# Moving the one-step recurrence and half of the key pages inside a hybrid decoder layer

## What is computed

```python
h = rmsnorm(x); z = h @ w_in                     # 25 column slots of 128, then the value and forget columns
# A: forgetting attention, 4 heads x 64; for the samples over 64 pages of 128 cached keys and values each
s = q @ k.T * 0.125 + c_q - c_k;  o_a = softmax(s) @ v        # c = running sum of the log forget gates
# B: RWKV-7 recurrence, 4 heads x 64, over the prompt in chunks and over the samples step by step
s_kk = sum_k(s * kk);  s = s * w - s_kk * (kk * a) + v * k;  o_b = sum_k(s * r)
o_b = group_norm(o_b) + bonus
# C: causal pooling, D: depthwise convolution module
y = rmsnorm(x + concat(o_a*silu(g_a), o_b*silu(g_b), o_c*silu(g_c), o_d*silu(g_d)) @ w_out)
```

## Time and profile before

| | us |
|---|---|
| median of 3 runs (1960.63 to 1970.27) | 1962.02 |
| the profiled execution | 1961.91 |
| its span from the first to the last instruction | 1960.1 |

### The profile page before, as it was taken

The page is one execution under the profiler, slowest core; times in us unless marked ns, Lnnn a source line. Parts: engine busy times, 40 slices in busy tenths (PEclk is TensorE's granted clock), DMA queues, the critical chain, the costliest instruction groups (busy, mean ns, idle before and its releaser), DMA issues.

```text
span 1960.1 us, 34623 instructions
## 1 busy us (share of the span) xinstructions
PE 1801.5 (92%) x14642; PEld 1092.4 (56%) x14642; DVE 817.9 (42%) x1662; ACT 478.5 (24%) x855; POOL 170.1 (9%) x220
## 2 busy tenths in 40 slices
PE   6999999999999999979999997887788786999997
PEld 3555555555554556746776775666667342444442
DVE  4450799732213350036556533444434864111112
ACT  4301100010526231125554531111112231100000
POOL 1000000011000005600000000000000001111110
PEclk9999999999999999989999998998989798999999
DMA  6222321385230535141100057777776536878782
GB/s 224 78 105 80 118 87 64 121 196 158 92 120 33 204 153 206 50 152 39 54 1 1 2 175 224 221 236 218 213 226 193 226 100 230 296 272 277 277 297 74
DMA packets 149269, 298.62 MB, mean 152 GB/s; under 512 B 23301, under 2 KB 119349, under 8 KB 130742
## 3 DMA queue, kind: packets, MB, share of 16 engines
q1 hardware_dynamic: 126602, 152.65, 24.7%
q0 software_dynamic: 18240, 115.82, 17.3%
q10 hardware_dynamic: 4272, 27.93, 3.6%
HBM read 234.66 MB, written 63.92 MB: 152 GB/s over the span
## 4 chain that ended last, share of the span: by engine, by line
PE 58%; DVE 17%; SPq 15%; issue 4%; DMA 3%; ACT 3%; POOL 0%; ACTq 0%; DVEq 0%
PE psum L756 23%; PE psum L1257 12%; SPq L525 12%; DVE big L1647 8%; PE psum L908 6%; PE psum L948 4%; PE psum L841 3%; PE psum L919 3%; PE psum L895 2%; SPq L521 2%; PE psum L788 1%; ACT big L1326 1%; PE psum L1242 1%; DMA rkv<-big 1%; DVE big L2029 1%
## 5 line engine op out<-in xcount | busy, mean ns | idle before, releaser
L756 PE MATMUL psum<-big,wbuf 128*128 128x416 f32 x1920 | 675.4, 513 | 3.9 <-DVE big L1577 3.4
L756 PEld LDWEIGHTS psum<-big,wbuf 128*128 128x128 f32 x1920 | 365.0, 190 | 310.7 <-issue 309.0
L948 PE MATMUL psum<-big 64*64 64x64 f32 (+2 forms) x6496 | 269.6, 281 | 48.8 <-DMA big<-in_k_pages 34.0
L948 PEld LDWEIGHTS psum<-big 64*64 64x64 f32 (+1 forms) x6496 | 190.0, 132 | 140.1 <-issue 69.5
L1295 ACT ACTIVATE zst<-psum 128x416 f32<-128x416 f32 x125 | 64.0, 516 | 540.7 <-PE psum L756 540.6
L1257 PE MATMUL psum<-big 128*128 128x512 f32 (+1 forms) x408 | 181.8, 595 | 0.0
L720 POOL DMA_INDIRECT big<-in_cache_v,pidx x64 | 60.7, 949 | 1027.2 <-PE psum L948 1020.5
L1647 DVE SCALAR_TENSOR_TENSOR big<-big,pars 128x2048 f32<-128x2048 f32 x120 | 148.2, 1298 | 1.1
L1257 PEld LDWEIGHTS psum<-big 128*128 128x128 f32 (+1 forms) x408 | 76.2, 187 | 101.4 <-issue 101.4
L2116 DVE TENSOR_TENSOR zst<-zst,psum 128x1024 f32<-128x1024 f32 (+1 forms) x17 | 20.7, 1221 | 224.5 <-PE psum L1257 224.5
L1555 ACT ACTIVATE big<-zst 128x1024 f32<-128x1024 f32 (+1 forms) x17 | 18.0, 1057 | 299.8 <-DVE zst L2116 299.8
(11 more groups left out here) (238 smaller groups left out, 1818.2 us busy)
## 6 DMA issues: line engine op xcount, KB each, us to landing
big<-in_k_pages SPq DMA_DIRECT2D x352, 128.0 KB, 2.3
zT<-zst ACTq DMA_DIRECT2D x25, 1040.0 KB, 6.5
zst<-in_k_pages SPq DMA_DIRECT2D x160, 128.0 KB, 2.4
wbuf<-in_w_slots SPq DMA_DIRECT2D x24, 512.0 KB, 4.5
big<-zT POOLq DMA_DIRECT2D x11, 1024.0 KB, 5.6
rwS<-big POOLq DMA_DIRECT2D x8, 1024.0 KB, 4.2
big<-rwS SPq DMA_DIRECT2D x8, 1024.0 KB, 5.9
zst<-in_x_prompt SPq DMA_DIRECT2D x16, 512.0 KB, 9.2
```

What stands on the lines that cost most here:

```text
L756: last = nc.tensor.matmul(psum[:, m % CHUNKS, 0:CW], w[:, k, :], hT[:, k, c * CW:(c + 1) * CW], start=(k == 0), stop=(k == KT - 1))
L948: return nc.tensor.matmul(out, l, r, start=start, stop=stop, skip_group_check=True)
```

## The change

**The recurrence of the samples** now runs inside the projection. The host hands the state over turned (`state_T`), so that the sum over k is a sum over partitions: `sample_step(i)` makes `s_kk` with 32 small products, whose stationary side is one column broadcast to 64x64, and the output of the step before with 32 products of one column. That is five calls: before the last piece of slot 23 and before value rows 0, 2, 4 and 6. VectorE keeps per step four operations of 128x1024, after four that prepare the values. The value rows of the samples are turned on TensorE after slot 21, copied by ScalarE in slot 22, stored by four ScalarE transfers to `zsD` and loaded, spread over 64 partitions, by SyncE. The keys and queries of attention are loaded after this is done, since they use the same memory. The value rows use PSUM banks 0 to 4 in place of 5 to 7.

**Half of the key steps** (16 of 32) now stand in attention, after items 6, 8, ..., 24 and then 25 to 30. They have one buffer (`k_early`, 2 MB), so that SyncE loads the next 16 pages when the step before has been scored. In the recurrence each pair keeps two steps, with the ring of three. To make room, the gates of attention come tile by tile: before item j+3 SyncE loads its 128x128 gate into one of four small buffers, and it stores the result of each item by itself. The queries of the samples are laid out at item 1 (`decode_queries`, at item 31 before), and the scans go to items 3, 11, 17, 19, 21, 23, 25 and 27.

**The tail** after the pairs: the norm comes first, piece by piece with both channel halves, so that `mixb_ready` rises ten times; two blocks of probabilities are turned after its first pass and six after its third, then ten value tiles run back to back. `project` takes the products of mixer B last.

```diff
+v_row = [area(HT + 13010 + i * 1024, 1024) for i in range(DEC_SEQ)]
+s_wkv = [area(HT + 17106, 1024), area(HT + 18130, 1024)]
+s_tmp = area(HT + 19154, 1024)
+v_turned = pars[0:SMP, 339:595].rearrange("p (h t x) -> p h t x", h=2, t=2)
+o_smp = sb("o_smp", [P, 2, SMP])
...
+KEYS_AT = (6, 8, 10, 12, 14, 16, 18, 20, 22, 24, 25, 26, 27, 28, 29, 30)
+SUMS_AT = (3, 11, 17, 19, 21, 23, 25, 27)
+KEARLY = len(KEYS_AT)
+KPAIR = (KSTEPS - KEARLY) // NPAIR
...
+    sp.wait_ge(v_spread, 16 * DEC_SEQ)
+    sp.dma_start(s_wkv[0], I['state_T']).then_inc(s_in, 16)
+    for i in range(DEC_SEQ):
+        sp.dma_start(v_row[i], zsD[i].unsqueeze(1).to_broadcast([2, 64, 1024])).then_inc(x_in[i], 16)
...
+    sp.wait_ge(s_done, 1)
+    sp.dma_start(O['wkvT_sample'], s_wkv[0]).then_inc(wkv_stored, 16)
+    sp.wait_ge(wkv_stored, 16)
...
+    def gate_store(j):
+        i, pr = ITEMS[j]
+        sp.wait_ge(o_read, j + 1)
+        sp.dma_start(mixT[MIX_A + pr][:, i * P:(i + 1) * P], gate_a[j % 4]).then_inc(mixa_stored[j % 2], 16)
+        if j + 3 < len(ITEMS):
+            if j > 0:
+                sp.wait_ge(mixa_stored[1 - j % 2], 16 * ((j + 1) // 2))
+            gate_load(j + 3)
...
+        if k < KEARLY:
+            if k > 0:
+                sp.wait_ge(sc_mm, k)
+        elif k - KEARLY >= NRING:
...
+    for j in range(len(ITEMS) - 2):
+        if j == 2:
+            key_pages(0)
+        if j in KEYS_AT and KEYS_AT.index(j) + 1 < KEARLY:
+            key_pages(KEYS_AT.index(j) + 1)
+        gate_store(j)
+        if j == 11:
+            for t in range(2):
+                sp.dma_start(O['kT'][t], zT[KA + t]).then_inc(st_stored, 16)
...
-        for j in range(4):
-            if n * 4 + j + NRING < KSTEPS:
-                key_pages(n * 4 + j + NRING)
+        for j in range(KPAIR):
+            if KEARLY + n * KPAIR + j + NRING < KSTEPS:
+                key_pages(KEARLY + n * KPAIR + j + NRING)
...
+    def sample_step(i):
+        if i == 0:
+            pe.wait_ge(lora_read, 21)
+            pe.wait_ge(s_in, 16)
...
+        if i < DEC_SEQ:
+            for b in range(DEC_BATCH):
+                for t in range(2):
+                    for h in range(2):
+                        hs, x = slice(h * 64, h * 64 + 64), b * DEC_SEQ + i
+                        last = nc.tensor.matmul(psum[hs, 5 + b // 4, (b % 4 * 2 + t) * 64:(b % 4 * 2 + t + 1) * 64],
+                                                smp[hs, 3, t, x:x + 1].to_broadcast([64, 64]), now[hs, b, t, :], start=True, stop=True, skip_group_check=True)
+            last.then_inc(sk_mm, 1)
+        if i > 0:
+            for b in range(DEC_BATCH):
+                for t in range(2):
+                    for h in range(2):
+                        hs, x = slice(h * 64, h * 64 + 64), b * DEC_SEQ + i - 1
+                        last = nc.tensor.matmul(psum[hs, 7, t * SMP + x:t * SMP + x + 1], now[hs, b, t, :], smp[hs, 0, t, x:x + 1],
+                                                start=True, stop=True, skip_group_check=True)
+            last.then_inc(so_mm, 1)
...
+            if n == 23 and c == 4:
+                sample_step(0)
...
+                if m in (0, 2, 4, 6):
+                    sample_step(1 + m // 2)
...
+        if c == 0 and j - 1 in KEYS_AT:
+            pe.wait_ge(sc_read, KEYS_AT.index(j - 1) + 1)
...
+    def early_keys(j):
+        k = KEYS_AT.index(j)
+        if k == 0:
+            pe.wait_ge(qbd_ready, 1)
+        pe.wait_ge(k_early_in, K_EARLY0 + 256 * (k + 1))
+        pe.wait_ge(o_read, j)
+        key_step(k, 6 + (j + 1) % 2, k_early)
...
-        keys(1)
         for l in range(1, 6):
             square(0, l)
             square(1, l)
-            if l in (2, 4):
-                keys(1 + l // 2)
+            if l == 2:
+                keys(1)
...
-    for i in range(DEC_SEQ):
-        for n in range(5):
-            k = i * 5 + n
-            pe.wait_ge(s_z, k + 1)
-            if k >= 3:
-                pe.wait_ge(s_used, k - 2)
-            for hf in range(2):
-                last = nc.tensor.matmul(psum[:, 2 * (k % 3) + hf, :], ones_head[:, :],
-                                        z_exp[:, n, hf * 512:(hf + 1) * 512], start=True, stop=True)
-            last.then_inc(s_mm2, 1)
...
-                if g % 3 == 0:
-                    value_tile(g // 3 - 1)
+        if k == 0:
+            turn_probs(0)
+            turn_probs(1)
+    for blk in range(2, 8):
+        turn_probs(blk)
+    pe.wait_ge(D['pT'], D0['pT'] + 16)
+    pe.wait_ge(D['p'], D0['p'] + 9)
+    transpose(psum[0:SMP, 6, 0:P], s_new[:, :]).then_inc(D['pT_tr'], 1)
+    pe.wait_ge(D['l_bc'], D0['l_bc'] + 1)
+    nc.tensor.matmul(psum[:, 7, 0:P], l_bc[:, :], ident[:, :], start=True, stop=True).then_inc(D['l_mm'], 1)
+    pe.wait_ge(D['pT'], D0['pT'] + 17)
+    for n in range(10):
+        value_tile(n)
...
-        for k, e in enumerate((2, 3, 0, 1, 4, 5, 6, 7)):
+        for k, e in enumerate((0, 1, 4, 5, 6, 7, 2, 3)):
+            if k == 6 and o == 0:
+                pe.wait_ge(mixb_ready, 2 * ((T * P + n - 1) // CW + 1))
...
+            if n == 22 and c == 1:
+                a_(smp[:, 1], smp[:, 1], ACT.Exp, s_dec)
+                act.wait_ge(lora_mm, 21)
+                a_(v_turned.rearrange("p h t x -> p t h x"), psum[0:SMP, 5, 0:256].rearrange("p (t h x) -> p t h x", t=2, h=2), ACT.Copy, lora_read)
+                act.wait_ge(lora_read, 21)
+                for i in range(DEC_SEQ):
+                    act.dma_start(zsD[i].rearrange("h (b x) -> b h x", x=P), pars[i:SMP:DEC_SEQ, 339:595].rearrange("b (h x) -> b h x", h=2)).then_inc(v_spread, 16)
...
+    for i in range(DEC_SEQ):
+        dve.wait_ge(x_in[i], X_SEEN[i] + 16)
+        ch.mark(v.tensor_tensor(shape(v_row[i]), shape(v_row[i]), column(2, i), ALU.mult))
+    dve.wait_ge(s_in, 16)
+    dve.wait_ge(s_dec, 1)
+    for i in range(DEC_SEQ):
+        old, new = s_wkv[i % 2], s_wkv[1 - i % 2]
+        if i >= 2:
+            dve.wait_ge(so_mm, i - 1)
+        ch.link(v.tensor_tensor(shape(new), shape(old), column(1, i), ALU.mult))
+        ch.link(v.tensor_tensor(new, new, v_row[i], ALU.add))
+        dve.wait_ge(sk_mm, i + 1)
+        ch.link(v.tensor_tensor(shape(s_tmp), shape(psum[:, 5:7, :].rearrange("p a b -> p (a b)")), column(4, i), ALU.mult))
+        v.tensor_tensor(new, new, s_tmp, ALU.subtract).then_inc(s_ready, 1)
+        dve.wait_ge(s_ready, i + 1)
+    dve.wait_ge(so_mm, DEC_SEQ)
+    v.tensor_copy(o_smp[:, :, :], psum[:, 7, 0:2 * SMP].rearrange("p (t x) -> p t x", t=2)).then_inc(s_done, 1)
...
+    def early_scores(j):
+        if j in KEYS_AT:
+            key_scores(KEYS_AT.index(j), 6 + (j + 1) % 2)
...
-            if 20 <= j < 28:
-                forget_sums(j - 20)
+            if j == 1:
+                decode_queries()
+            if j in SUMS_AT:
+                forget_sums(SUMS_AT.index(j))
```

More of the change, by code:

```diff
@@ L202, in build @@
         gc_in = sem("gc_in")
-        gates = sem("gates")
         glu_ready = sem("glu_ready")
@@ L836, in value_rows @@
                     pe.wait_ge(pars_in, 32)
-                    pe.wait_ge(lora_read, 20)
-                if n >= 3:
-                    pe.wait_ge(vf_evac, n - 2)
+                if n < CHUNKS:
+                    pe.wait_ge(z_evac, done[0] - CHUNKS + n + 1)
+                else:
+                    pe.wait_ge(vf_evac, n - CHUNKS + 1)
                 for k in range(KT):
-                    last = nc.tensor.matmul(psum[0:r, 5 + n % 3, 0:VF], hT[:, k, n * P:n * P + r], wvf[:, k, :], start=(k == 0), stop=(k == KT - 1))
+                    last = nc.tensor.matmul(psum[0:r, n % CHUNKS, 0:VF], hT[:, k, n * P:n * P + r], wvf[:, k, :], start=(k == 0), stop=(k == KT - 1))
@@ L842, in value_rows, with turn_samples @@
                 last.then_inc(vf_mm, 1)
+            def turn_samples():
+                pe.wait_ge(made, IDENT)
+                pe.wait_ge(rk_in, 64)
+                pe.wait_ge(lora_read, 20)
+                for t in range(2):
+                    last = transpose(psum[0:SMP, 5, t * P:t * P + P], smp[:, 5, t, :])
+                last.then_inc(lora_mm, 1)
+            def sample_step(i):
+                if i == 0:
+                    pe.wait_ge(lora_read, 21)
+                    pe.wait_ge(s_in, 16)
+                    pe.wait_ge(s_dec, 1)
+                    pe.wait_ge(L_ready, 4)
+                else:
+                    pe.wait_ge(s_ready, i)
+                now = s_wkv[i % 2].rearrange("p (b t v) -> p b t v", b=DEC_BATCH, t=2)
+                if i < DEC_SEQ:
+                    for b in range(DEC_BATCH):
+                        for t in range(2):
+                            for h in range(2):
[5 more added lines that the diff above has]
+                    for b in range(DEC_BATCH):
+                        for t in range(2):
+                            for h in range(2):
[3 more added lines that the diff above has]
+                    last.then_inc(so_mm, 1)
@@ L923, in values, with key_step @@
```

(24 more changed lines are left out.)

307 lines of the change are left out of this document (118 added, 189 removed).

## The result

The changed kernel takes 1929.97 us (median of 4, 1928.07 to 1936.35) where the kernel before takes 1965.84 on the same chip: ratio 0.983, 95% interval [0.980, 0.985]. That is a gain of some 36 us; 98 were forecast, and 1929.97 lies outside the range of 1836 to 1900. The profiled execution has a span of 1926.3 us against 1960.1 before, 33.8 less.

A forecast was written before the change was run, and what follows sets the result against it. TensorE was taken to bound projection, attention and output projection, SyncE's issue of key pages the pairs. Pairs -104, attention +39, projection +15, tail -48 make -98 from 1961.91, so 1864 us; range 1836 to 1900.

The forecast's parts named there:

- Pairs: Recurrence over pairs: two of four key steps leave, page waits vanish, period 32.0 us; -104 us, bounds -87 to -109.
- (a): Rival: small ScalarE and VectorE copies hold pairs at 34.5 us or more, sample steps at 60 ns; 1897 us, chance 0.26.
- Tail: After the pairs: with the sample recurrence gone, the output projection starts at +72.5 instead of 120.4; -48 us.
- Projection: Sample steps moved into the projection add small TensorE products; +15 us, bounds +10 and +38.
- No wait, or up to 8 us if the loads are late: Projection: VectorE finishes sample step 0 at about 763, when TensorE is about to ask for it.
- one-column products would be cheaper: Projection: possible lower cost of the sample steps' products, 8 us in all instead of 15.
- Attention: Attention takes sixteen key steps, a stall behind stores, and moved queries and scans; +39 us, bounds +28 and +58.
- The stall behind the stores: Attention, key step after item 14: its pages queue behind seven stores; 7.7 us plus about 1 of slow clock, +9.
- +4 - 5 + 1: Attention: queries and a scan in early items +4, scans leaving items 20 to 27 -5, `values` waiting for key scores +1.
- (c): Rival: slow page issues make the single key buffer stall each of 15 attention steps; near 2010 us, chance 0.03.
- (d): Rival: pairs stay near 44 us because what SyncE waits for sets the pace; 1968 us, chance 0.03.
- (b): Rival: better than forecast, with fast gathers, hidden stall behind the stores and cheap one-column products; 1839 us, chance 0.18.

The follow-up runs named there:

- s3_banks: e1_sixteen with the eight turned probability blocks written alternately to PSUM banks 6, 7 and 4, 5; ratio 0.964 on a slower chip.
- e1_sixteen: Changed kernel with each of the four sample value-row loads written as two, one per half of the partitions; 1884.97 us, ratio 0.960.
- s4_again: The kernel of s4_all run once more, on a chip where the kernel before takes 1963.46 us; 1854.53 us, ratio 0.943.
- s1_stores: e1_sixteen with the seven output stores spread over items 13 to 21 instead of in a row after item 11; ratio 0.960, slower chip.
- u1_keys: Changed kernel with all key steps back in the pairs, four a pair, none in attention; ratio 0.993 on a slower chip.
- s2_ckrest: e1_sixteen with the 3 MB `ck_rest` load issued only after the projection's last store landed; single run, attention 345.9 us.
- s4_all: e1_sixteen plus spread stores, `ck_rest` after the projection's last store, and turned blocks in two bank pairs; 1930.43 us, ratio 0.953, slower chip.
- s5_all_three: s4_all with 8 key steps in attention and three a pair; ratio 0.955 on a slower chip.
- s6_late: s4_all with the 64 log forget gate gathers started only after the last value row, key steps from item 10 on; 1862.31 us, ratio 0.946.

## Why the prediction was right or wrong

**Pairs, right.** -97.2 against -104, inside the bounds. The period is 33.2 us and not 32.0; undoing the part brings 44.8 back. No page is waited for. The 6.8 us between lie in gaps in which TensorE waited for nothing that the profile shows: 18.4 us here, 8.9 before. Their cause is open. They vary with the run: with two steps a pair the stage took 265.7 to 276.9 us in ten traces, 265 being the forecast. The copies of VectorE and ScalarE, my rival (a), cost 4 us in all.

**Tail, right, but two steps were off and cancelled.** From the end of the pairs (1539.3 + 1.5 = 1540.8, the instant that was 1526.4 before) the third norm pass ended at +31.7 (forecast +35), the six turned blocks at +49.1 (+50), the output projection started at +73.3 (+72.5), and the last things waited for were gathers. The passes were 3.3 us shorter than forecast. The six blocks took 17.4 us and not 15, since four of them ran at the low clock, a block every 3.2 us and not 2.4. That both sizes were off by nearly as much in opposite directions is luck. s3_banks confirms the chain: the six blocks take 8.0 us there, 9.4 less, and the stage is 8.8 shorter.

**Projection, wrong: "No wait, or up to 8 us if the loads are late".** The work was sized nearly right. The sample rows on TensorE cost 16.9 us against 15, and 15.4 without the slow row behind the wait. Counted from the same point of the program (624 us in the kernel before), e1_sixteen and s4_again, which don't wait, are 18.3 us longer to the start of attention. Most of the 2.9 beyond the rows lies in the value rows behind the last step, where the clock was 0.96 from 800 to 841 in e1_sixteen, against 1.00 over the value rows before. That one-column products would be cheaper (8 us in all) didn't come, nor did 60 ns an instruction: each took about 30 ns, as the nearest row had said. The step that failed is "State and values, 2.5 MB, can be issued from 739.5 and land by about 755". I had priced the loads by their bytes at the rate of other loads, and hadn't looked at their shape. Four of five ran at 41 GB/s, and the last landed at 799.5. 38.5 us of waiting, 1.5 of slow row, 3.3 of work beyond the 15 and 0.6 that the kernel was late at 625 us already make the largest part of the miss: 44 of 64 us. The sign for it had been named: a wait of TensorE for `s_ready` near 760. It stands there, from 767 to 805.7.

**Attention, wrong in size.** The mechanisms were there; what each cost, from the times at which VectorE finishes the 32 items in five kernels: the steps themselves 27.7 us (s1_stores less u1_keys, 324.3 - 296.6 from item 0 to 31; forecast 30). The stall behind the stores 16.6 (forecast 9, of which its 7.7 are 7.5 by its own instants): the place was right, the key step after item 14, but TensorE was there 17.3 us after item 11 and not 20, and the pages landed 31.6 and not 27.5 us after it. Decoded queries and moved scans +5.4 (u1_keys less the kernel before, 296.6 - 291.2): of the forecast +4 - 5 + 1 the gain of 5 didn't come, since a scan that leaves one item stands on the chain of another (items 11, 17 and 19 became 2.4 us longer each in u1_keys). And +3.2 at the start, where I had nothing: `ck_rest` is issued ahead of the last store of the projection. I had named the queue past which the keys move, but not that of this load, which the diff moves without touching its line, by taking the gate loads from in front of it. -0.3 for the rest.

**Rivals.** (c), the single key buffer, decides nothing: but for the stores no step waited over 0.5 us for its pages, with 8.1 to 9.7 us for 16 issues. (d) is refuted by the pairs. (b), 1839, came about in no run; of its parts only the hidden stall came, in the repaired version, 1854.5. Of (a) neither part came: the period is 33.2 us, under its 34.5.

## What to carry to other kernels

Price a load by the shape of its pattern before its bytes: a broadcast written with the small dimension outside ran at 41 GB/s, the same bytes with 64 partitions outside at over 220. Where work moves into a stage that a queue serves, write down the issues of that queue in their order around each new deadline; both further losses were a transfer behind other transfers, and both went by reordering alone. When one engine's queue sets the pace (44.8 us a pair for four steps), moving part of its work pays until the next limit, here 33 to 35 us for two or three.

## What the runs showed that I had not expected

A load on few engines holds the issuing queue as well: SyncE stood 29.6 us on four issues, 5.3 on eight of the other shape. Here nothing urgent was behind them.

A store of 1 MB that is issued 0.5 us behind a load of 3 MB landed after 9.9 us; in front of it by 0.3 us, in the kernel before, after 6.7; with the load held back until it had landed, in s2_ckrest, after 3.9.

The chips differ in one stretch. On the two chips where the kernel before takes 2028 us, TensorE got a sample product only every 0.7 to 2.8 us between about 757 and 841, in all six kernels traced there, with nothing to wait for that the profile shows; 56.8 us in s1_stores. Two of the six have a longer gap besides, of 12.1 us (s4_all) and 7.9 us (s5_all_three). Start, duration and idle time before:

```profile
818.83 0.26 PE L911 MATMUL psum<-big,smp 64*64 64x64 f32 x1 [2.54 <-issue]
821.63 0.26 PE L911 MATMUL psum<-big,smp 64*64 64x64 f32 x1 [2.54 <-issue]
824.43 0.26 PE L911 MATMUL psum<-big,smp 64*64 64x64 f32 x1 [2.54 <-issue]
```

In the DMA view of the stretch of 785 to 838 of s1_stores there are only 39 of the 64 gathers of log forget gates and the rest of one store; the queue that brings instructions has no packet. In e1_sixteen, on another chip, it has three from 785 to 824, and there are no such gaps; but TensorE had got further in its program there, so the packets may be a consequence. The gaps of 2.5 us end at 835.6, about when the gathers' last bytes move. In u1_keys it also hits the full-size products of the projection, one every 2.8 us. So on such a chip the repaired loads are worth little: u1_keys, with the slow ones, ends the projection at 950.4, s1_stores at 948.3. That the gathers cause it was only argued: the run made to tell, s6_late, fell on a chip without it, and of the kernel before no trace exists from a chip with it. That TensorE waited for its own instructions, as the text before s6_late says, is a reading too. It stays open.
